# Two-layer model on one core: the mixture of experts on 24 groups of 32 token slots in column tiles, with the weights as the moving operand

## What is computed

```python
def swiglu(x, wg, wu, wd):
    return (jax.nn.silu(x @ wg) * (x @ wu)) @ wd

def moe(x, router, wg, wu, wd):
    logits = (x @ router).astype(jnp.float32)
    top_logit, top_idx = lax.top_k(logits, TOP_K)
    top_w = jax.nn.softmax(top_logit, axis=-1)
    gates = jnp.sum(jax.nn.one_hot(top_idx, N_EXPERTS, dtype=jnp.float32) * top_w[..., None], axis=-2)
    y = jnp.zeros_like(x)
    for e in range(N_EXPERTS):
        y = y + gates[..., e:e + 1].astype(x.dtype) * swiglu(x, wg[e], wu[e], wd[e])
    return y

# in the first block, layer 1 (i = 1):
        u = rmsnorm(h, norm_ffn[i])
            h = h + moe(u, router[j], exp_w_gate[j], exp_w_up[j], exp_w_down[j])
        ple = p[i] @ w_ple[i]
        h = h + jax.nn.sigmoid(rmsnorm(h, norm_ple[i]) @ w_ple_gate[i]) * ple
```

## Time and profile before

| | |
|---|---|
| time, median of 3 runs | 2768.66 us (2767.34 to 2768.82) |
| profiled execution, span of the core | 2763.8 us; its own time isn't recorded, the span is 4.9 us under the median |
| TensorE busy | 2679.6 us, 97% |
| DVE busy | 1415.0 us, 51% |
| ACT busy | 511.7 us, 19% |
| loads read from memory | 472.71 MB, 171 GB/s over the span |
| share of the 16 DMA engines taken by the loads' queue | 48.3% |

### The profile page before, as it was taken

How to read it: one execution, slowest core, us unless ns; L and a number is a source line. 1 busy time by engine, 2 the same in 40 slices (tenths; PEclk the granted TensorE clock), 3 DMA queues, 4 the chain that set the end, 5 groups by cost and what they waited for, 6 DMA issues and landing times.

```text
span 2763.8 us, 42355 instructions
## 1 busy us (share of the span) xinstructions
PE 2679.6 (97%) x18752; PEld 2314.3 (84%) x18752; DVE 1415.0 (51%) x1850; ACT 511.7 (19%) x818; POOL 157.8 (6%) x143
## 2 busy tenths in 40 slices
PE   8999999999999999999999999999999999998998
PEld 5878888999778788896969758795899988767998
DVE  4773323886568432252324100258568777685554
ACT  1272111110116211010100000123211122122111
POOL 0002210000000231000000000000000010100000
PEclk9999999999999999999999999999999999999999
DMA  7442214886443321157574678634279634441442
GB/s 266 137 148 92 77 46 146 319 320 232 135 167 125 111 73 62 50 198 254 181 269 166 251 297 296 222 122 153 69 282 356 230 124 136 151 141 61 168 169 91
DMA packets 212357, 476.49 MB, mean 172 GB/s; under 512 B 8016, under 2 KB 37328, under 8 KB 211920
## 3 DMA queue, kind: packets, MB, share of 16 engines
q1 hardware_dynamic: 211600, 472.27, 48.3%
q10 hardware_dynamic: 576, 1.52, 0.2%
HBM read 472.71 MB, written 1.05 MB: 171 GB/s over the span
## 4 chain that ended last, share of the span: by engine, by line
PE 89%; DVE 6%; ACT 2%; DMA 2%; issue 1%; SPq 0%; POOL 0%; DVEq 0%; ACTq 0%
PE ps L1809 22%; PE ps L484 16%; PE ps L557 11%; PE ps L549 8%; PE ps L2010 5%; PE ps L2057 4%; PE ps L2325 3%; PE ps L2426 2%; PE ps L1218 2%; PE ps L1229 2%; PE ps L2353 1%; PE ps L1225 1%; PE ps L2499 1%; PE ps L2691 1%; DVE work L1470 1%
## 5 line engine op out<-in xcount | busy, mean ns | idle before, releaser
L484 PE MATMUL ps<-uT,ring 128*128 128x256 f32 x1024 | 232.7, 382 | 12.0 <-DMA ring<-in_w_in 9.3
L484 PEld LDWEIGHTS ps<-uT,ring 128*128 128x128 f32 x1024 | 191.9, 192 | 37.4 <-issue 9.3
L1809 PE MATMUL ps<-uT,ring 128*128 128x128 f32 x1584 | 186.8, 276 | 2.6 <-ACT uT L945 1.9
L1809 PEld LDWEIGHTS ps<-uT,ring 128*128 128x128 f32 x1584 | 182.2, 192 | 4.9 <-issue 3.7
L484 PE MATMUL ps<-xn,ring 128*128 128x256 f32 x768 | 175.6, 388 | 10.1 <-issue 7.5
L1809 PE MATMUL ps<-xn,work 128*128 128x128 f32 x1584 | 179.8, 275 | 0.0
L1809 PEld LDWEIGHTS ps<-xn,work 128*128 128x128 f32 x1584 | 178.3, 192 | 0.0
L484 PEld LDWEIGHTS ps<-xn,ring 128*128 128x128 f32 x768 | 147.4, 195 | 31.7 <-issue 11.7
L557 PEld LDWEIGHTS ps<-uT,ring 128*128 128x128 f32 x1344 | 155.8, 194 | 6.8 <-issue 6.2
L557 PE MATMUL ps<-uT,ring 128*128 128x128 f32 x1344 | 157.9, 277 | 2.3 <-ACT uT L945 2.3
L1859 ACT ACTIVATE work<-ps 128x512 f32<-128x512 f32 (+1 forms) x108 | 60.3, 559 | 399.0 <-PE ps L1809 399.0
(11 more groups left out here) (486 smaller groups left out, 4527.5 us busy)
## 6 DMA issues: line engine op xcount, KB each, us to landing
ring<-in_w_in SPq DMA_DIRECT2D x72, 1024.0 KB, 5.1
work<-in_ada_w SPq DMA_DIRECT2D x48, 1024.0 KB, 10.8
ring<-in_attn_w_in SPq DMA_DIRECT2D x36, 1024.0 KB, 5.2
ring<-in_exp_w_gate SPq DMA_DIRECT2D x32, 1024.0 KB, 8.0
ring<-in_ffn_w_in SPq DMA_DIRECT2D x32, 1024.0 KB, 7.4
ring<-in_exp_w_down SPq DMA_DIRECT2D x31, 1024.0 KB, 6.2
ring<-in_ffn_w_out SPq DMA_DIRECT2D x22, 1024.0 KB, 7.9
ring<-in_exp_w_up SPq DMA_DIRECT2D x20, 1024.0 KB, 8.7
```

Of the source, the lines that this page charges most:

```text
L484: mm = pe.matmul(acc[:, m * T:(m + 1) * T], w[:, k, m * P:(m + 1) * P], src[:, half * 4 + k, :], start=(half == 0 and k == 0 and m % 2 == ...
L1809: mm = pe.matmul(acc[:, m * P:(m + 1) * P], weights[:, k, m * P:(m + 1) * P], x[:, k, :], start=(start and m == 0 and k == 0), stop=True, ...
```

## The change

All eight experts now go the packed way. The 512 rows are put in 24 units of 32 slots (768 slots), in six passes of four units; the four units of a pass are the column tiles. The 24 units are cut into 12 jobs of 4, 3, 3, 2, 2, 2, 2, 2, 1, 1, 1 and 1 units (`PASS_JOBS`). A job reads one set of weights. Which expert takes which jobs depends on the loads: a table, computed on the host from constants only, holds a plan per row with the capacity of each rank; the first row whose capacities hold all loads is chosen on the chip (a comparison with `caps`, a small product that counts the fitting rows before, and a product that picks the row). The eight largest ranks' first jobs are loaded from memory; the other four jobs of an expert that has more than one are copied inside SBUF, two by ACT, two by DVE.

The stage is 70 steps. For each group of 512 (twice) or 384 columns of the inner width there are eight steps of gate and eight of up, one for each 128 rows of the input; then eleven steps for the left 512 columns of the down part and eleven for the right. A step needs 128 rows of each of the eight matrices: eight loads of 128 x 512 (256 KB; 192 KB with 384 columns). There are three sets of buffers of 3 MB, two in the ring's place and one in `work`. SP loads a set again when the step three before has been multiplied. Register addresses say where in the set an expert's weights land (`first_job`) and which copies are made (`extra_jobs`).

At the end of each gate phase ACT applies silu to the six banks, at the end of each up phase DVE multiplies; the hidden rows are transposed during the steps that follow. Rows are brought back for the left 512 columns during the right down phase, for the right ones at the end. The `ple` product is split in two halves around the choice of the plan. After the stage, a slab's place is loaded again only when the last step that used its set is done.

```diff
+UNIT = 32
+PASS_JOBS = ((4,), (3, 1), (3, 1), (2, 2), (2, 2), (2, 1, 1))
+PASSES = len(PASS_JOBS)
+JOB_SIZES = tuple(n for of in PASS_JOBS for n in of)
+JOBS = len(JOB_SIZES)
+JOB_OF = tuple(j for j, n in enumerate(JOB_SIZES) for _ in range(n))
+N_UNITS = len(JOB_OF)
+N_SLOTS = N_UNITS * UNIT
+N_PLAN = 2 * N_UNITS + EXPERTS + 2 * (JOBS - EXPERTS)
+SET = JOBS * 512
...
-        N_WIDE, SOLO, PACKED, UNIT = 3, (3, 4), (5, 6, 7), 32
-        PACKS = (((5, 0), (5, 1), (5, 2), (6, 0)), ((6, 1), (6, 2), (7, 0), (7, 1)))
...
+        UP_PHASES = 2 * len(GROUPS)
+        STEPS = [(ph, k) for ph in range(UP_PHASES) for k in range(KT)] + [(UP_PHASES + h_, k) for h_ in range(2) for k in range(FE)]
+        DOWN_L, DOWN_R = UP_PHASES, UP_PHASES + 1
+
+        def last_k(ph):
+            return (KT if ph < UP_PHASES else FE) - 1
+
+        def step_width(ph):
+            return GROUPS[ph // 2] * P if ph < UP_PHASES else 512
+
...
+        job_sets = [ring.rearrange("p r c -> p (r c)")[:, 0:SET], ring.rearrange("p r c -> p (r c)")[:, SET:2 * SET], area(0, SET)]
+        SETS = len(job_sets)
...
+        def step_done(eng, s):
+
+            ph, k = STEPS[s]
+            if k == last_k(ph):
+                eng.wait_ge(moe_acc, acc_done(ph, PASSES - 1))
+            else:
+                eng.wait_ge(moe_used, s + 1 - ph)
...
+            ple_half_pe(pe, 1, 0)
+            acc = take_unit(pe, "plan")
+            pe.wait_ge(rt_fit, 1)
+            pe.matmul(acc[:, 0:1], before, fits, start=True, stop=True).then_inc(tick(psum_full), 1)
+            pe.wait_ge(rt_fit, 2)
+            pe.matmul(acc[:, 512:512 + N_PLAN], chosen, col("plan"), start=True, stop=True).then_inc(tick(rt_plan), 1)
+            ple_half_pe(pe, 1, 1)
...
+            pick_pe(pe, 0)
+            pick_pe(pe, 1)
+            for s, (ph, k) in enumerate(STEPS):
+                step_pe(pe, s, ph, k)
+                if ph == 0 and k + 2 < KT:
+                    pick_pe(pe, k + 2)
+                elif ph == 1 and 1 <= k <= 3:
+                    put_turn_pe(pe, k - 1)
+                elif ph in (2, 4, 6) and 1 <= k <= PASSES:
+                    hidden_turn_pe(pe, ph // 2 - 1, k - 1)
+                elif ph == DOWN_R and 1 <= k <= 8:
+                    put_left_pe(pe, k - 1)
+            put_right_pe(pe)
+            slab_n[0] += 1
+            extra[0] -= 1
...
+        def step_pe(pe, s, ph, k):
+            g, w = ph // 2, step_width(ph)
+            buffers = job_sets[s % SETS].rearrange("p (j c) -> p j c", c=512)
+            pe.wait_ge(job_in[s % SETS], 16 * EXPERTS * (s // SETS + 1))
+            pe.wait_ge(job_dve, 2 * (s + 1))
+            pe.wait_ge(job_act, 2 * (s + 1))
+            if ph == 0:
+                pe.wait_ge(pick_act, k + 1)
+                pe.wait_ge(pick_dve, k + 1)
+                tokens = packed[:, k, :]
+            elif ph < UP_PHASES:
+                tokens = packed[:, k, :]
+            else:
+                group = next(i for i in range(len(GROUPS)) if k < sum(GROUPS[:i + 1]))
+                if ph == DOWN_L and k == sum(GROUPS[:group]):
+                    pe.wait_ge(hidt_act, 3 * (group + 1))
+                    pe.wait_ge(hidt_dve, 3 * (group + 1))
+                tokens = hid_t[group][:, k - sum(GROUPS[:group]), :]
+            for i in range(PASSES):
+                if k == 0:
+                    if ph == 0 and i == 4:
+                        pe.wait_ge(pick_act, 2)
+                        pe.wait_ge(pick_dve, 2)
+                    elif ph == DOWN_R:
+                        evicted(pe, 0, i)
+                    elif ph % 2:
+                        pe.wait_ge(moe_sil, PASSES * g + i + 1)
+                    elif ph:
+                        pe.wait_ge(moe_hid, PASSES * (g - 1) + i + 1)
+                for j in range(4):
+                    u = 4 * i + j
+                    mm = pe.matmul(bank_of(i)[j * UNIT:(j + 1) * UNIT, 0:w], tokens[:, u * UNIT:(u + 1) * UNIT],
+                                   buffers[:, JOB_OF[u], 0:w], start=(k == 0), stop=(k == last_k(ph)),
+                                   skip_group_check=True, tile_position=(0, j * UNIT))
+                if k == last_k(ph):
+                    mm.then_inc(tick(moe_acc), 1)
+            if k != last_k(ph):
+                mm.then_inc(tick(moe_used), 1)
...
+        def put_right_pe(pe):
+            pe.wait_ge(h_new, 4 * (H_BEFORE["ple1"] - 1) + 1)
+            for n in range(4):
+                for i in range(PASSES):
+                    if n == 0:
+                        evicted(pe, 1, i)
+                    mm = pe.matmul(right_acc(n), y_rows[:, i, 512 + n * P:512 + (n + 1) * P], put[:, i, :],
+                                   start=(i == 0 and n != 1), stop=(i == PASSES - 1), skip_group_check=True)
+                if n:
+                    mm.then_inc(tick(y_part), 1)
+
...
+        def job_copies_act(act, s, regs):
+            ph, _ = STEPS[s]
+            w, buffers = step_width(ph), job_sets[s % SETS]
+            act.wait_ge(job_in[s % SETS], 16 * EXPERTS * (s // SETS + 1))
+            for src, dst in regs:
+                act.activation(buffers[:, bass.ds(dst * 512, w)], buffers[:, bass.ds(src * 512, w)], ACT.Copy).then_inc(tick(job_act), 1)
...
+        def extra_jobs(eng, c0, c1):
+
+            eng.wait_ge(rt_idx, 1)
+            at = [eng.value_load(job_at[0:1, 8 + c:9 + c], min_val=0, max_val=JOBS - 1) for c in (c0, c1, 4 + c0, 4 + c1)]
+            return ((at[0], at[2]), (at[1], at[3]))
...
+                if ph < UP_PHASES and ph % 2 == 0 and k == last_k(ph):
+                    for i in range(PASSES):
+                        act.wait_ge(moe_acc, acc_done(ph, i))
+                        w = step_width(ph)
+                        act.activation(hidden[:, i, 0:w], bank_of(i)[:, 0:w], ACT.Silu).then_inc(tick(moe_sil), 1)
...
-                    if j0 + first in halved_slabs():
-                        sp.wait_ge(pk_half, steps_done - 2)
-                        for j, (r, piece) in step:
-                            ffn_load(sp, expert(r), (n + j0 + j) % R, piece, gate, up, down, 0)
-                        for j, (r, piece) in step:
-                            sp.wait_ge(slab_used, n + j0 + j - R + 1)
-                            if piece[0] != "d" or piece[2] == 2:
-                                ffn_load(sp, expert(r), (n + j0 + j) % R, piece, gate, up, down, 1)
-                        continue
...
+            first_job = [sp.value_load(job_at[0:1, e:e + 1], min_val=0, max_val=JOBS - 1) for e in range(EXPERTS)]
+            sp.wait_ge(slab_used, n)
+            for s, (ph, k) in enumerate(STEPS):
+                if s >= SETS:
+                    step_done(sp, s - SETS)
+                for e in range(EXPERTS):
+                    dst = job_sets[s % SETS][:, bass.ds(first_job[e] * 512, step_width(ph))]
+                    sp.dma_start(dst, moe_source(ph, k, e)).then_inc(job_in[s % SETS], 16)
...
+        def moe_source(ph, k, e):
+
+            if ph < UP_PHASES:
+                c0 = sum(GROUPS[:ph // 2]) * P
+                return ins[("exp_w_gate", "exp_w_up")[ph % 2]][0][e, k * P:(k + 1) * P, c0:c0 + step_width(ph)]
+            return ins["exp_w_down"][0][e, k * P:(k + 1) * P, (ph - DOWN_L) * 512:(ph - DOWN_L + 1) * 512]
```

More of the change, by code:

```diff
@@ L2245, in build @@
[L2245 to L2248 removed]
+        z0 = columns["ret0"][0]
+        assert columns["mg6"][0] + P - z0 >= 3 * N_SLOTS
@@ new lines, in build @@
+        packed = area(6, KT * N_SLOTS).rearrange("p (k s) -> p k s", s=N_SLOTS)
+        y_rows = area(6, PASSES * D).rearrange("p (i d) -> p i d", d=D)
+        hidden = area(12, PASSES * 512).rearrange("p (i c) -> p i c", c=512)
+        hid_t = [xu[:, 0:4 * N_SLOTS], area(15, 4 * N_SLOTS), small[:, z0:z0 + 3 * N_SLOTS]]
+        hid_t = [x.rearrange("p (a s) -> p a s", s=N_SLOTS) for x in hid_t]
+        put = area(18, PASSES * T).rearrange("p (i t) -> p i t", t=T)
+        plb1 = area(19.5, 2048)
@@ new lines, in build, with bank_of, spare, acc_done @@
+        SETS = len(job_sets)
+        def bank_of(i):
+            return ps[i // 2][:, i % 2 * 512:i % 2 * 512 + 512]
+        def spare(i):
+            return ps[3][:, i * 512:(i + 1) * 512]
+        def acc_done(ph, i):
+            return PASSES * ph + i + 1
+        def by_dve(i):
+            return i in (2, 3)
+        def evicted(eng, half, i):
+            n = sum(by_dve(j) == by_dve(i) for j in range(PASSES))
+            before = sum(by_dve(j) == by_dve(i) for j in range(i))
+            eng.wait_ge(y_dve if by_dve(i) else y_act, n * half + before + 1)
@@ new lines, in hidden_turn_pe @@
+        def hidden_turn_pe(pe, g, i):
+            pe.wait_ge(moe_hid, PASSES * g + i + 1)
+            if i % 2 == 0:
+                if g + i == 0:
+                    pe.wait_ge(put_act, 2)
+                else:
+                    pe.wait_ge(hidt_act, 3 * g + i // 2)
+            elif g + i == 1:
+                pe.wait_ge(put_dve, 1)
+            else:
```

(22 more changed lines are left out.)

838 lines of the change are left out of this document (300 added, 538 removed).

## The result

The changed kernel takes 2603.95 us, the median of four runs (2601.12 to 2606.59); the kernel before took 2768.0 us in the four runs beside them. The ratio is 0.9412 with a 95% interval of 0.9398 to 0.9425: 164 us or 5.9% faster, and 25 us slower than forecast. Run again beside the experiments it took 2602.79 us, ratio 0.9405 (0.9389 to 0.9420).

A forecast was written before the change was run, and what follows sets the result against it. TensorE bounded the old stage; loads were to bound the new one. A 380 us stream from 1191.8 us, plus the end, puts the next product at 1584.5 instead of 1774.5: 2768.7 - 190 = 2579 us, range 2553 to 2618.

The forecast's parts named there:

- the stream: Weight loads of the rewritten expert stage: 560 transfers, 138.4 MB, forecast to take 380 us (bounds 358 and 416).
- the bound: In the rewritten expert stage the limit was to move from TensorE to the loads, with TensorE busy about half.
- 172 us, or 2.6 us a step: TensorE time of the 70 gate, up and down steps, 24 matmuls each; 2.0 us at 384 columns.
- TensorE has 206 us of work: Sum of steps, gathers, transposes and bring-back products in the expert stage, where TensorE had 584 us before.
- So loads never wait for a set: Three weight buffer sets: release to reuse takes 11.3 us, three sets allow 17.1; at half clock 13.9.
- The end: Close of the stage: last bytes 1571.6 us, then copies, products, eviction, 18 right-hand products; 1583.5 taken, plus 1 us charged.
- The clock. TensorE will be busy 2.6 us and idle 3 us: Expert stage: clock low for much of it, a mixture of half and full, hidden by the loads.
- Hidden either way: SBUF copies of doubled experts' weights in each step: between nothing and 1.4 us, hidden at either size.
- B: Rival: clock stays at half and TensorE paces the expert stage, 422 us instead of 380; kernel 2621 us; chance 0.11.
- C: Rival: the stage's transfers run like the 4 KB-packet ones, 404 GB/s, stream 343 us; kernel 2542 us; chance 0.10.
- D: Rival: small transfers don't overlap their fixed part; if each is paid alone, stage 1,570 us, kernel 3,750; chance 0.03.
- E: Rival: three buffer sets serve as one, a step costs 11.3 us, stage 790 us, kernel 2,970; chance 0.02.

## Why the prediction was right and wrong

**Right: the direction and the stream; half right: the bound.** The loads now run nearly without a pause, but TensorE's time bounds the stage as much as theirs: it was busy 395 of 411 us, where the prediction had about half, with a wait at nearly each step. The stream came out as worked out, once little held it: 382 us from the first load to the last bytes in the kernel with four passes, against 380 and 1.8 us of start. The first load at 1188.74 us (forecast 1190), the shares near 1 and 363 GB/s in 1256 to 1395 (forecast 355 to 375) are the changed kernel's own. Part of that agreement is luck. The steps of 512 columns, 5.40 us for 2.10 MB (388 GB/s), were faster than the 369 forecast; those of 384 columns took 4.65 us in the mean (1379.58 to 1449.35 for 15 steps, 338 GB/s) where 347 were forecast, and there were pauses where phases change.

**The step that failed** is "172 us, or 2.6 us a step", and with it "TensorE has 206 us of work". It is a term of the sum that came out at half its size, since two records of the trace belong to one matmul. Measured: 54 steps of 5.29 us and 16 of 4.0 us are 350, four gathers in 10.56 us make 21 for eight, the left half 12.5, the right 10.6, transposes 13: about 407 us, and 395 of them stand in the window of 411. Transposes alone stand as one record each and were right (12.1 forecast). What followed from it:

- "So loads never wait for a set" failed. The way of a set was worked out as 11.3 us of 17.1; with 5.3 us of products it is 14, and with a gather 16.8. The shares of 0.79 and 0.93 at the two ends are loads that waited. With four of six passes they waited little (0.99 over the stage, 0.94 with the gathers), and the kernel took 2576.57 us, 2.4 us from the forecast of 2579: so the size of TensorE's work accounts for the miss.
- "The end": the last bytes landed at 1600.6 instead of 1571.6 us, 29 us late. Beside the kernel with four passes it was 15 us behind at the last up step of 512 columns (1390.33 against 1375.37); 8 of these came with the gathers (1256.30 against 1248.15), where a step took TensorE 8.07 us. Another 12 came in the down parts, the right one at 6.78 us a step. From there to the gate product 19.2 us passed instead of 12.9: a step and the right half cost twice as much, and the prediction took 18 products for the right half where the code has 24. That is 35 us in the trace. The stages behind that point took 4.3 us less than before. And the forecast added 4.9 us, as the profiled execution before was that much under the median, while the changed kernel's was 0.9 us over it (2604.8 beside 2603.95), together 5.8. 35.3 less 4.3 less 5.8 are the 25 us of the miss. The sum is good to some 7 us: in the second trace the gate product starts at 1612.34 instead of 1619.85.
- "The clock. TensorE will be busy 2.6 us and idle 3 us" failed for the same reason: with 5.3 us of products in a step, and transposes or gathers behind many, there was hardly a gap. The mechanism itself is real. It shows where products are left out, behind most gaps of 2.6 to 4.4 us: a step of 7.0 to 7.9 us whose set comes back late. That is more than the forecast had, since the whole step is twice as long. The Trainium skill (TensorE: Matmul & The Clock Gate, HAM oscillation) tells of bursts between DMA waits that run cold; the kernels with half of the products and with one pass agree (0.88 and 0.67), the one with four passes of six does not run cold.
- "Hidden either way" of the copies failed by 10 us. With a step of 2.6 us they would have had room; no kernel here shows it.

That the time stayed within 25 us of the forecast, with TensorE's work at twice its size, is largely luck: a step's 5.29 us of products happen to lie just under the 5.40 us of its loads. Smaller slips change nothing: with its own bounds of 358 and 416 us for the stream the range is 2557 to 2615, not 2553 to 2618, and the 1,460 us for 560 loads are 1,437 if the 128 smaller ones are taken at their size.

The Trainium skill could have warned. FP8 and Floating Point Precision, TensorE Precision Notes, says that true FP32 takes four passes through the array (of the data, not the six passes of this kernel). By an estimate from this page, if a column takes one cycle and four column tiles run side by side, 4 x 512 columns at 2.4 GHz are 0.85 us for the four tiles of one of the kernel's passes and 5.1 us for six; the trace has 5.29 and agrees. The prediction's 108 ns for a matmul would have been four tiles in 0.43 us, half of that.

**The rivals.** B (TensorE paces, 2621) was nearest in kind: it had TensorE's work at 422 us by a halved clock, and it was about 407 us by the count of products at full clock. Its reason was wrong, its bound half right, since TensorE does pace the two ends. C (404 GB/s, 2542) fell: even with four passes the steps of 512 columns ran at 388 GB/s and no more, and the stage had 355. D fell, 560 transfers came at 0.68 us each (382 / 560) and not at a price of single ones. E fell: the three sets work as three, with shares above 1.

**Left open.** With half of the loads the stage ended at 1597 us, with four of six passes at 1588; with all of both it ends at 1612 to 1620. The copies account for 10 of the 15 to 23 us above the larger. That the rest comes from phases with different bounds, which three sets don't smooth, is argued and not shown; a fourth set was not tried.

## What to carry to other kernels

Before a mean time per record is multiplied with a count of instructions, the count in the trace is to be held against the count in the code at one known place; here it is a factor of two for the float32 products that were counted, and one for the transposes. Where two resources come out within a tenth of each other, as here with 407 and 382 us, neither is the answer alone: the phases take turns, and the time was above both. Work taken from TensorE in lumps moved nothing that could be told from no change (2599.51 us, clock 0.88), while less of it taken evenly gave 26 us (2576.57 us, clock 0.98).

## What the runs showed of the hardware that was not expected

- The granted clock went with how TensorE's idle time was spread. Busy 109.94 of 139 us, in bursts of about 4 us, it had 0.98; busy 104.98 of 139 (some of it at the lower clock), with full and nearly empty steps by turns, 0.88.
- Queued loads of 256 KB in 2 KB packets ran at 388 GB/s for several steps in a row, close to the 392 of 1 MB loads. Those of 192 KB in 1.5 KB packets came to 338 GB/s over their 15 steps in the kernel with four passes.
- A copy inside SBUF took 0.42 us on DVE in the median of all steps (most have 512 columns), against 0.69 for 512 columns out of PSUM; on ACT it was 0.61 against 0.59.
- A register read ahead of each of eight loads stretched their issue from 3.8 us (the third set's in the changed kernel) to 7.6 us, half a microsecond each.
